# Sliding window attention with one more unit in flight, in a one-core two-block kernel

## The reference

```python
h = jnp.concatenate([meta, x], axis=1)                 # 16 meta tokens + 1024
h = h + 0.5 * swiglu(rmsnorm(h, ffn1_norm), ...)
hn = rmsnorm(h, mix_norm)
q, k, v, u, g_attn, g_ssm = jnp.split(hn @ w_in, SPLITS, axis=-1)
attn = sliding_window_attention(q, k, v, attn_sinks)   # 16 heads of 64, 4 kv heads
y = jax.nn.gelu(s5_ssm(u, ...))
ssm = (y @ ssm_glu_a) * jax.nn.sigmoid(y @ ssm_glu_b)
merged = jax.nn.sigmoid(g_attn) * attn + jax.nn.sigmoid(g_ssm) * ssm
h = h + merged @ w_out
```

## Time and profile before

| what | us |
|---|---|
| median of 3 runs (3720.83 to 3725.34) | 3720.89 |
| the profiled execution, its own time | 3720.84 |
| its span | 3719.0 |
| TensorE busy in the span | 3566.3 (96%) |
| VectorE busy | 1435.6 (39%) |
| ScalarE busy | 957.7 (26%) |
| GpSimd busy | 1123.0 (30%) |

### The profile page before, as it was taken

One profiled execution on the slowest core, in us unless ns is written; L12 is line 12 of the kernel. 1 busy time (PEld: TensorE's weight loads), 2 busy tenths in 40 slices (PEclk: granted clock), 3 DMA queues, 4 the chain that ended last, 5 costly groups with the idle time before them and its releaser, 6 DMA issues.

```text
span 3719.0 us, 52408 instructions
## 1 busy us (share of the span) xinstructions
PE 3566.3 (96%) x20104; PEld 2949.9 (79%) x20104; DVE 1435.6 (39%) x2514; ACT 957.7 (26%) x1678; POOL 1123.0 (30%) x1503
## 2 busy tenths in 40 slices
PE   7998889999999999999999999998889999999998
PEld 4787777888888878899999878886667778888886
DVE  3297555211112163322122563737667431111114
ACT  4244433211111142111111332125553321111112
POOL 3142135322222253222222432310004542222223
PEclk9999999999999999999999999999999999999999
DMA  2111122111111121111111321111014221111113
GB/s 98 40 52 40 51 74 85 58 50 44 52 41 50 43 77 54 48 45 46 45 46 44 115 81 64 46 35 35 24 55 161 91 68 46 51 40 51 46 48 98
DMA packets 79301, 217.46 MB, mean 58 GB/s; under 512 B 18849, under 2 KB 18977, under 8 KB 78497
## 3 DMA queue, kind: packets, MB, share of 16 engines
q1 hardware_dynamic: 60960, 171.25, 15.3%
q10 hardware_dynamic: 18176, 43.93, 3.2%
HBM read 194.62 MB, written 19.46 MB: 58 GB/s over the span
## 4 chain that ended last, share of the span: by engine, by line
issue 61%; POOL 23%; PE 10%; DVE 3%; ACT 1%; DMA 1%; POOLq 1%; SPq 0%; ACTq 0%; DVEq 0%
POOL w_lo L556 23%; PE acc L689 2%; PE acc L690 2%; PE acc L691 2%; PE acc L1223 0%; POOLq L560 0%; DVE cv_acc L1698 0%; PE acc L1218 0%; DVE acc L1776 0%; DVE x_up L1779 0%; PE acc L603 0%; DMA x<-in_x_dram 0%; PE acc L1354 0%; PE acc L1310 0%; PE acc L1346 0%
## 5 line engine op out<-in xcount | busy, mean ns | idle before, releaser
L556 POOL TENSOR_TENSOR w_lo<-w_raw,w_hi 128x256 fp32r<-128x256 f32 (+3 forms) x1472 | 1084.2, 767 | 2467.2 <-ACT w_hi L526 2466.9
L689 PE MATMUL acc<-h_hi,w_hi 128*128 128x512 f32 (+1 forms) x3552 | 1317.0, 371 | 27.0 <-POOL w_lo L556 19.6
L690 PE MATMUL acc<-h_lo,w_hi 128*128 128x512 f32 (+1 forms) x3552 | 1315.8, 370 | 0.0
L691 PE MATMUL acc<-h_hi,w_lo 128*128 128x512 f32 (+1 forms) x3552 | 1310.0, 369 | 0.0
L689 PEld LDWEIGHTS acc<-h_hi,w_hi 128*128 128x128 f32 x3552 | 671.0, 189 | 156.7 <-issue 20.3
L690 PEld LDWEIGHTS acc<-h_lo,w_hi 128*128 128x128 f32 x3552 | 670.1, 189 | 119.5 <-issue 1.9
L691 PEld LDWEIGHTS acc<-h_hi,w_lo 128*128 128x128 f32 x3552 | 671.2, 189 | 116.9
L526 ACT CAST w_hi<-w_raw 128x1024 fp32r<-128x1024 f32 (+3 forms) x368 | 344.0, 935 | 1242.5 <-PE acc L691 1223.4
L969 DVE TENSOR_TENSOR ff_hi<-tmp,acc 128x512 f32 (+3 forms) x154 | 94.5, 614 | 1101.1 <-PE acc L691 1065.6
L689 PE MATMUL acc<-ff_hi,w_hi 128*128 128x512 f32 (+1 forms) x1232 | 450.1, 365 | 5.4 <-POOL w_lo L556 2.9
L691 PE MATMUL acc<-ff_hi,w_lo 128*128 128x512 f32 (+1 forms) x1232 | 447.7, 363 | 0.0
(11 more groups left out here) (361 smaller groups left out, 2982.0 us busy)
## 6 DMA issues: line engine op xcount, KB each, us to landing
w_raw<-in_ffn_w_dram SPq DMA_DIRECT2D x94, 512.0 KB, 3.5
w_raw<-in_w_in_dram SPq DMA_DIRECT2D x58, 512.0 KB, 3.5
w_raw<-in_w_out_dram SPq DMA_DIRECT2D x32, 512.0 KB, 3.5
w_raw<-in_ffn_w_dram SPq DMA_DIRECT2D x48, 320.0 KB, 2.9
w_raw<-in_w_gate_dram SPq DMA_DIRECT2D x24, 512.0 KB, 3.6
w_raw<-in_w_up_dram SPq DMA_DIRECT2D x24, 512.0 KB, 3.5
w_raw<-in_ffn_w_dram SPq DMA_DIRECT2D x32, 384.0 KB, 3.0
gates_kept<-gstage ACTq DMA_DIRECT2D x32, 256.0 KB, 2.0
```

Source lines behind the costliest of these rows:

```text
L556: pool.tensor_tensor(w_lo[:, j, a:a + step], w_raw[:, j, a:a + step], w_hi[:, j, a:a + step].bitcast(F32), ALU.subtract).then_inc(split_do ...
L689: pe.matmul(bank, wh, rh, start=(k == 0), stop=False)
L690: pe.matmul(bank, wh, rl, start=False, stop=False)
L691: ins = pe.matmul(bank, wl, rh, start=False, stop=(k == seg.kt - 1))
```

## The change

It has these parts.

1. Depth. TensorE's round does `values(u-3)`, `scores(u)`, `turn(u-2)`. VectorE's round does `outputs(u-3)`, `mask_max(u)`, `probabilities(u-1)`: the mask of a unit stands ahead of the scaling of the unit before it. ScalarE's round does `copies(u-3)`, the chunks, `exps(u-1)`.
2. The score buffer `sc` has three parts in place of two, and the PSUM bank that takes a unit's values is the other one of the pair (`at_bank`). The waits follow.
3. The last slab of `at_h` (16 pieces, chunks 14 and 15) is held back: the rounds 0 to 63 do 112 pieces, and the three rounds after them 6, 5 and 5.
4. `y_hi` and `y_lo` are made tile by tile in those last rounds: they wait for the last scores (`at_s`) in place of the last output. The first three tiles are spread over the rounds 64 to 66; the evacuation of chunks 14 and 15 stands on ScalarE behind the fourth tile, the other four tiles behind that, and the load of the stored gates behind those.
5. Placement in SBUF: `sc`, `pt`, `st`, `gstage`, `y_lo`, `gld` and `gtmp` move. `gstage` no longer shares room with a table of the state space part, and VectorE's wait for the stored gates ahead of `c_power(0)` is gone.

The core of the diff:

```diff
+SCORES = 3
+BEHIND = (6, 5, 5)
-        y_lo = place("y_lo", W + 16 * col, [P, 4, L], F32R)
-        gld = place("gld", W + 83328, [P, 2, 2, L])
+        y_lo = place("y_lo", W + 77312, [P, 4, L], F32R)
+        gld = place("gld", W + 93952, [P, 2, 2, L])
...
         def at_bank(u):
-            return 2 * ((u + 1) % 2)
+            return 2 * (u % 2)
...
         def gates_of(u):
-            total, n = GATE_CHUNKS * KD, len(UNITS)
-            return [divmod(g, KD) for g in range(total * u // n, total * (u + 1) // n)] if u < n else []
+            n = len(UNITS)
+            total = GATE_CHUNKS * KD - sum(BEHIND)
+            if u < n:
+                first, last = total * u // n, total * (u + 1) // n
+            else:
+                first, last = total + sum(BEHIND[:u - n]), total + sum(BEHIND[:u - n + 1])
+            return [divmod(g, KD) for g in range(first, last)]
...
-            for u in range(len(UNITS) + 2):
+            for u in range(len(UNITS) + 3):
                 for piece in gates_of(u):
                     gate_piece(piece)
-                if u >= 2:
-                    values(u - 2)
+                if u >= 3:
+                    values(u - 3)
                 if u < len(UNITS):
                     scores(u)
-                if 1 <= u <= len(UNITS):
-                    turn(u - 1)
+                if 2 <= u < len(UNITS) + 2:
+                    turn(u - 2)
...
+            for u in range(len(UNITS) + 3):
+                if u >= 3:
+                    copies(u - 3)
+                if u < len(UNITS):
+                    gates_out(u)
+                if 1 <= u <= len(UNITS):
+                    exps(u - 1)
+                if u >= len(UNITS):
+                    merged_high(0, u - len(UNITS))
+            merged_high(0, 3)
+            for u in range(len(UNITS), len(UNITS) + 3):
+                gates_out(u)
+            for ct in range(4):
+                merged_high(1, ct)
...
-            for s in range(2):
-                dve.wait_ge(sem(f"gate_stored{s}"), 16 * 2 * GATES_A)
             c_power(0)
...
-            for u in range(len(UNITS) + 2):
-                if u < len(UNITS):
-                    mask_max(u)
-                if u >= 2:
-                    outputs(u - 2)
-                if u < len(UNITS):
-                    probabilities(u)
+            for u in range(len(UNITS) + 3):
+                if u >= 3:
+                    outputs(u - 3)
+                if u < len(UNITS):
+                    mask_max(u)
+                if 1 <= u <= len(UNITS):
+                    probabilities(u - 1)
+                if u >= len(UNITS):
+                    merged_low(0, u - len(UNITS))
+            merged_low(0, 3)
+            for ct in range(4):
+                merged_low(1, ct)
```

More of the change, by code:

```diff
@@ L386, in build_program @@
         KW = META + 2 * P
-        sc = place("sc", W + 91648, [P, 2, 2 * KW])
-        pt = place("pt", W + 96000, [P, 2, 2, 384])
-        st = place("st", W + 102144, [P, 2, 5, 2])
+        sc = place("sc", W + 93952, [P, SCORES, 2 * KW])
+        pt = place("pt", W + 100480, [P, 2, 2, 384])
+        st = place("st", W + 106624, [P, 2, 5, 2])
         et = place("et", W + 4 * col, [P, 4, SC, 2, P])
@@ L400, in build_program @@
         prod_b = [place(f"prod_b{r}", W + 16 * col + r * 2048, [P, PAIRS, 32]) for r in range(2)]
-        gstage = place("gstage", W + 102272, [P, 2, 512])
+        gstage = place("gstage", W + 106720, [P, 2, 512])
         y_hi = place("y_hi", W + 12 * col, [P, 4, L], F32R)
-        y_lo = place("y_lo", W + 16 * col, [P, 4, L], F32R)
-        gld = place("gld", W + 83328, [P, 2, 2, L])
-        gtmp = place("gtmp", W + 83328 + 4 * col, [P, 3, 512])
+        y_lo = place("y_lo", W + 77312, [P, 4, L], F32R)
+        gld = place("gld", W + 93952, [P, 2, 2, L])
+        gtmp = place("gtmp", W + 66560, [P, 3, 512])
         acc = ctx.enter_context(nc.psum_tensor("acc", [P, 8, 512], F32))
@@ L1966, in probs @@
             kw = unit(u)[3]
[L1967 removed]
+            return sc[:, u % SCORES, KW - kw:KW] if hd == 0 else sc[:, u % SCORES, KW:KW + kw]
         ET_BANK = (2, 5, 6)
         def at_bank(u):
[L1973 removed]
+            return 2 * (u % 2)
         def at_chunk(f):
@@ L2093, in scores @@
                     pe.wait_ge(sem("at_masked"), u - 1)
-                if u >= 3:
-                    pe.wait_ge(sem("at_oc"), u - 2)
+                if u >= 4:
+                    pe.wait_ge(sem("at_oc"), u - 3)
                 band = kw - META
@@ L2110, in turn @@
                     pe.wait_ge(sem("at_ptc"), u)
-                pe.transpose(acc[0:2 * META, 4, 0:nq], sc[:, u % 2, KW - META:KW + META], ident)
+                pe.transpose(acc[0:2 * META, 4, 0:nq], sc[:, u % SCORES, KW - META:KW + META], ident)
                 for hd in range(2):
@@ L2114, in turn @@
                         a, at_ = 384 - (kw - META) + k * P, (KW - kw, KW + META)[hd] + k * P
-                        ins = pe.transpose(acc[:, 4 + hd, a:a + nq], sc[:, u % 2, at_:at_ + P], ident)
+                        ins = pe.transpose(acc[:, 4 + hd, a:a + nq], sc[:, u % SCORES, at_:at_ + P], ident)
                 ins.then_inc(sem("at_pt"), 1)
@@ L2121, in values @@
                 pe.wait_ge(sem("at_ptc"), u + 1)
-                if u + 1 < len(UNITS):
-                    pe.wait_ge(sem("at_masked"), u + 2)
+                if u + 2 < len(UNITS):
+                    pe.wait_ge(sem("at_masked"), u + 3)
                 else:
@@ L2262, in copies, with gates_out @@
                 act.copy(pt[:, b, :, a:384], acc[:, 4:6, a:384]).then_inc(sem("at_ptc"), 1)
-            for u in range(len(UNITS) + 1):
+            def gates_out(u):
                 for f, k in gates_of(u):
@@ L2270, in act_mix2, with merged_high @@
                             w_after(act, seg, i, j)
-                if u:
-                    copies(u - 1)
-                if u < len(UNITS):
-                    exps(u)
+            def merged_high(c, ct):
+                c0, w = CH1[c]
+                act.wait_ge(sem("at_s"), len(UNITS))
+                act.copy(token_view(y_hi[:, ct, c0:c0 + w]), by_token(ct, c0, w)).then_inc(sem("y_hi_full"), 1)
+            for u in range(len(UNITS) + 3):
+                if u >= 3:
+                    copies(u - 3)
+                if u < len(UNITS):
+                    gates_out(u)
[8 more added lines that the diff above has]
+                merged_high(1, ct)
             act.wait_ge(sem("at_oc"), len(UNITS))
-            for c0, w in CH1:
-                for ct in range(4):
-                    act.copy(token_view(y_hi[:, ct, c0:c0 + w]), by_token(ct, c0, w)).then_inc(sem("y_hi_full"), 1)
             for s in range(2):
@@ L2464, in mask_max @@
                 hp, cols, nq, kw = unit(u)
-                b = u % 2
+                b, k = u % 2, u % SCORES
                 dve.wait_ge(sem("at_s"), u + 1)
-                if u >= 2:
-                    dve.wait_ge(sem("at_pt"), u - 1)
+                if u >= SCORES:
+                    dve.wait_ge(sem("at_pt"), u - SCORES + 1)
                 mask_ = const("band")
@@ L2476, in mask_max @@
                                                       ALU.mult, ALU.add))
-                    own.mark(dve.tensor_scalar(sc[:, b, KW:KW + META], acc[:, 2 * b + 1, 0:META], 0.125, None, ALU.mult))
-                    ins = dve.scalar_tensor_tensor(sc[:, b, KW + META:KW + kw], acc[:, 2 * b + 1, META:kw], 0.125,
+                    own.mark(dve.tensor_scalar(sc[:, k, KW:KW + META], acc[:, 2 * b + 1, 0:META], 0.125, None, ALU.mult))
+                    ins = dve.scalar_tensor_tensor(sc[:, k, KW + META:KW + kw], acc[:, 2 * b + 1, META:kw], 0.125,
                                                    mask_[:, META + P:KW], ALU.mult, ALU.add)
@@ L2482, in mask_max @@
                 own.wait()
-                own.link(dve.tensor_reduce(st[0:nq, b, 0, :], sc[:, b, KW - kw:KW + kw].rearrange("p (a k) -> p a k", a=2), AX_X, ALU.max))
+                own.link(dve.tensor_reduce(st[0:nq, b, 0, :], sc[:, k, KW - kw:KW + kw].rearrange("p (a k) -> p a k", a=2), AX_X, ALU.max))
                 stt(st[0:nq, b, 0, :], st[0:nq, b, 0, :], -1.0, neg_sinks[0:nq, 2 * hp:2 * hp + 2], ALU.mult, ALU.min)
@@ L2503, in outputs, with merged_low @@
                 dve.tensor_copy(q2[:, hp, cols], acc[:, at_bank(u), 384:384 + nq]).then_inc(sem("at_oc"), 1)
-            for u in range(len(UNITS) + 2):
+            def merged_low(c, ct):
+                c0, w = CH1[c]
+                dve.wait_ge(sem("y_hi_full"), 4 * c + ct + 1)
+                dve.tensor_tensor(token_view(y_lo[:, ct, c0:c0 + w]), by_token(ct, c0, w),
+                                  token_view(y_hi[:, ct, c0:c0 + w].bitcast(F32)), ALU.subtract).then_inc(sem("y_split"), 1)
+            for u in range(len(UNITS) + 3):
+                if u >= 3:
+                    outputs(u - 3)
                 if u < len(UNITS):
                     mask_max(u)
-                if u >= 2:
```

(5 more changed lines are left out.)

## The result

| | us |
|---|---|
| before, median of 4 runs (3716.65 to 3725.34) | 3720.86 |
| changed, median of 4 runs (3678.38 to 3681.67) | 3678.99 |
| ratio, 95% interval | 0.989 (0.9878 to 0.9902) |
| forecast | 3684 (3674 to 3703) |

What follows compares the result with a forecast made beforehand. A ring of VectorE and ScalarE's exponentials was taken to set the 4.15 us round. Rounds 263.1 to 218.2 (-44.9) and drain 27.4 to 35.1 (+7.7) give -37.2 from 3720.8: 3684 us, range 3674 to 3703.

Steps and rivals of the forecast that it cites:

- TensorE's need of 3.61 us: Attention rounds: TensorE's own work, 4.15 less 0.54 us, sets a two-piece round once the wait for VectorE is gone.
- the prediction's 40.2: Rounds: TensorE idle time removed, 29.5 us in 55 rounds, 6.3 in the first 8, 4.4 at 0.07 a round.
- 11.2 for the pieces: Rounds: 16 pieces fewer, at 0.70 us each, shorten the rounds by 11.2 us; that work moves to the drain.
- the late copies: One-piece rounds: copies to pt end at 1.5 us, values due at 1.35; 0.2 us in 14 rounds, 2.8 us.
- Rounding and GpSimd's split: Seven rounds with weight rounding: ScalarE's overrun costs 3.2 us, GpSimd's split slowing VectorE costs 2.0 (bounds 0 and 4.2).
- exclusive lock: Rounds: VectorE and GpSimd operations exclude each other by the skill's rule, up to 19.6 us; 2.0 taken from the rows.
- T + 5.1: Drain, T being the first glu matmul: ScalarE ends y_hi then loads gates; they land near T + 9.6, second pair T + 16.3.
- the 2.0 us for the clock: Drain: TensorE's idle time ahead of the second glu pair brings the slow clock, 1.5 to 2.9 us, taken as 2.0.
- A: Rival, rounds: another engine binds, meetings with VectorE and ScalarE leave rounds of 3.85 us, 23 us more, 3707; chance 0.17.
- C: Rival, rounds: no change; late mask and scaling keep transposes waiting, round near 4.04 us, 3721; chance 0.03.
- D: Rival, rounds: slower; a ring through the output copy closes in one round, 123 us more, 3844; chance 0.04.
- B: Rival, drain: gates land at T + 19.9 and clock costs 2.9, 3688; with VectorE's combining slowed, 3693; chance 0.12.

Runs made afterwards that it cites:

- scores first: Changed kernel with scores(u) ahead of values(u-3) on TensorE and VectorE's output copy between mask and maximum; 3675.1 us, ratio 0.9869 to 0.9902.
- sigmoid first: Changed kernel with the sigmoid of the first gates ahead of ScalarE's wait for the last y_lo; 3679.6 us, ratio 0.9877 to 0.9910.
- longer exponentials: Four more small operations in a row in ScalarE's exponentials of a unit: 3783.7 us in the kernel before, 3685.5 us in the changed kernel.
- none held back: Changed kernel with all 128 pieces in rounds 0 to 63 and none behind them; 3680.0 us, ratio 0.9880 to 0.9913.
- depth alone: Changed kernel with no piece held back and all y_hi and y_lo behind the last output as before; 3682.6 us, ratio 0.9883 to 0.9916.

## Why the prediction was right

**The bound.** It held: TensorE's need of 3.61 us, taken as 4.15 less 0.54, is the measured round, and 2.91 for one piece is that of scores first. Of the 35.8 us of idle time that the rows show ahead of the transposes (29.5 and 6.3) 2.1 remain. The other 4.4 of the prediction's 40.2 were worked out from modelled ends of matmuls; the round of 3.61 bears them out.

**The terms of the rounds.** The prediction took off 11.2 for the pieces and put back 2.8 for the late copies, which gives 8.4; the runs with and without holding back differ by 8.5. The copies end 1.5 us behind the transposes, as summed. Rounding and GpSimd's split had 3.2 and 2.0. Six rounds stand over 3.61, by 0.50, 0.28, 0.27, 0.27, 0.46 and 0.45, together 2.2 us (start to start of the transposes), so these two terms were too large by 3 us together. The sum was 218.2 against 216.8, too large by 1.4 only, so the other terms were 1.6 too small and part of the agreement is luck; no run reads them apart. The exclusive lock of which the Trainium skill speaks ("SBUF — State Buffer", section "Who interferes with whom") could by the prediction's estimate have cost up to 19.6 us; all that stands over 3.61 in the changed kernel's rounds is the 2.2.

**The drain.** The prediction had 16.8 us to the first glu matmul, and 16.75 were measured. Behind it stands the step that was mis-sized: "ScalarE ... ends `y_hi` at T + 5.1 and only then loads the gates". `y_hi` did end at T + 5.0, but the load was issued at T + 1.9: the copies ahead of it did not hold it up. The trace of before has the same (last section), and could have been read so. With the gates 3 us earlier their load was off the path, and the table load and the sigmoid behind the last `y_lo` set it: the second pair came 14.66 us behind the first glu matmul in place of 16.3. It came 6.2 us behind the sigmoid's start (2742.61), as the prediction had it. So the idle time ahead of the second pair was 1.46 and not 3.8 us, and the clock stayed at 1.00 behind it, so that the 2.0 us for the clock were not paid. The drain took 31.4 in place of 35.1. With 1.4 from the rounds this is the difference between 37.2 and 42.3. It is shown by the rows above and by sigmoid first, which took the 1.46 us away.

**The rivals.** A (a round of 3.85) did not come, though VectorE waits at the scores 0.47 us a round and so has about as little room as I gave it. From 2576 to 2686 us the rounds with two pieces and no rounding of weights are 3.60 to 3.63 us long. As priced, A would have given 3707, outside of the stated range of 3674 to 3703 that was to hold it. C and D are excluded by the rounds and by the longer exponentials. B did not come for the gates of the first sigmoid, which were issued 4.8 us ahead of `x`. The next load of gates, at 2741.95, did lie beside `x`: the second sigmoid waited 3.52 us for it, to 2751.59, behind the end of the stretch.

## What to carry to other kernels

When an engine waits once a round for the same thing, write down the ring: which engine's operations lie between two starts of it, and whose work of this round it needs. Work taken from an engine that only waits for such a ring gains next to nothing (16 pieces: 1.5 of 11.2 us) until the ring spans two rounds; after that it counts. When a buffer is added, ask which ring it breaks by itself: here the order was worth some 27 us with two buffers, and the third brought 15 more (both over the stretch, with the drain's parts: 290.5, 263.4, 248.3).

## What the runs showed of the hardware that I had not expected

A transfer issued from ScalarE's queue did not wait for the operations ahead of it in ScalarE's program, once its own semaphores were reached: in the changed kernel the gates' load was issued at 2736.03 with 3.1 us of copies still to be done. In the trace of before 8.2 us were left (the eight tiles of `y_hi` run from 2773.90 to 2782.22 and stand ahead of the load):

```profile
2773.98 0.83 ACTq L2284 DMA_DIRECT2D gld<-gates_kept  x2
...
2776.95 5.27 ACT L2278 CAST y_hi<-u 128x512 fp32r<-128x512 f32 x5
```

Idle TensorE time lowered the clock in some cases and not in others. With 2.0 us of work in the 4 us from 2724 (none held back), and behind idle times of 1.46 us, it stayed at 1.00. With 1.14 us of work in the 4 us from 2732 (depth alone) it was at 0.79 in that window and at 0.50 in the next. The window of none held back:

```profile
2724.00:2728.00 4.00, 2.02 (x25) 1.55 (x27) 3.65 (x13) 3.72 (x10) 0.41 (x2) 1.00 0.22 66
```

The same wait does not always do the same: behind the wait of 2.8 us in the later layer the clock stayed at 1.00 in three traces (before, none held back, changed with longer exponentials) and fell in the eleven others.
